# Hybrid attention and expert-retrieval step on one core: the planner that spreads the front's steps gives the choice of keys six row times instead of four

## The reference, cut to what matters

```python
h = rms(x)
cq, ckv, kpe, bq, bk, bv, iq, iw, ik, ga, gb = split(h @ w_in)
# mixer A: latent attention, 8 heads; mixer B: an indexer scores the keys, the best 128 of a prompt row are kept
score = einsum('bqh,bqhs->bqs', iw, relu(einsum('bqhd,bsd->bqhs', iq, ik)))
_, sel = top_k(where(mask, score, -inf), k_sel)
x = x + (sigmoid(ga) * (o_a @ w_o_a) + sigmoid(gb) * (o_b @ w_o_b)) @ w_out
# PEER: 8 heads, each takes 16 of 128*128 experts; u[e], v[e] are rows of 1024
a = gelu(einsum('td,thkd->thk', t, u[e]))
x = x + einsum('thk,thkd->td', g * a, v[e])
```

## Time and profile before

| | |
|---|---|
| time before, median of 3 runs | 1802.56 us (1797.75 to 1805.56) |
| the profiled execution's own time | 1796.99 us |
| its span | 1795.2 us |
| PE busy | 68% of the span |
| DVE busy | 73% |
| ACT busy | 32% |
| POOL busy | 29% |
| moved by DMA | 696.48 MB |

### The profile page before, as it was taken

How to read it: one execution, slowest core, us unless ns; L and a number is a source line. 1 busy time by engine, 2 the same in 40 slices (tenths; PEclk the granted TensorE clock), 3 DMA queues, 4 the chain that set the end, 5 groups by cost and what they waited for, 6 DMA issues and landing times.

```text
span 1795.2 us, 26399 instructions
## 1 busy us (share of the span) xinstructions
PE 1223.4 (68%) x9056; PEld 679.3 (38%) x9056; DVE 1310.8 (73%) x3857; ACT 579.7 (32%) x1995; POOL 526.2 (29%) x569
## 2 busy tenths in 40 slices
PE   8989976677867575878877666679867343434343
PEld 3668532344535232444535223356535111111111
DVE  5662696989666676989666768998766878686754
ACT  2331134333423333334323334344423222222222
POOL 0200232333322223332322223232323333333332
PEclk9989889787988696897998697887999555555555
DMA  6238699999999999999999999999999999999997
GB/s 267 74 100 294 250 422 421 422 425 425 424 424 423 417 401 383 420 425 424 425 423 422 423 407 390 426 400 398 422 424 423 427 426 426 425 427 423 427 421 294
DMA packets 119381, 696.48 MB, mean 388 GB/s; under 512 B 17983, under 2 KB 21118, under 8 KB 49102
## 3 DMA queue, kind: packets, MB, share of 16 engines
q0 software_dynamic: 78848, 570.53, 76.0%
q1 hardware_dynamic: 36686, 121.83, 17.5%
q10 hardware_dynamic: 3712, 2.43, 0.4%
HBM read 691.65 MB, written 3.02 MB: 387 GB/s over the span
## 4 chain that ended last, share of the span: by engine, by line
DMA 35%; DVE 25%; PE 25%; issue 6%; ACT 3%; POOL 1%; ACTq 0%; DVEq 0%; SPq 0%; POOLq 0%
DMA rows<-in_peer_uv,index 26%; DVE rows L2657 11%; PE ps_v L1820 5%; DMA wch<-in_w_row 4%; PE ps_f L1559 4%; PE ps_f L1353 2%; PE ps_f L1574 2%; PE ps_h L1800 2%; DMA wch<-in_peer_wq 2%; DVE score L2333 1%; PE ps_f L1477 1%; PE ps_f L1653 1%; DVE best L2332 1%; DMA wch<-in_w_ukv 1%; PE ps_f L1437 1%
## 5 line engine op out<-in xcount | busy, mean ns | idle before, releaser
L2657 DVE CUSTOM_DVE_ANT_0 rows<-rows,ps_h 128x1024 f32<-128x1024 f32 x544 | 658.0, 1220 | 289.1 <-DMA rows<-in_peer_uv,index 236.3
L1330 POOL DMA_INDIRECT rows<-in_peer_uv,index x544 | 516.4, 949 | 1169.4 <-PE ps_v L1820 988.8
L1820 PE MATMUL ps_v<-rows,diag 128*32 128x256 f32 x4352 | 419.1, 500 | 432.0 <-ACT diag L2164 424.8
L1820 PEld LDWEIGHTS ps_v<-rows,diag 128*32 128x32 f32 x4352 | 124.2, 130 | 677.5 <-ACT diag L2164 561.7
L2155 ACT ACTIVATE tan<-arg 128x2 f32<-128x2 f32 x272 | 55.3, 203 | 799.2 <-DVE arg L2667 756.4
L2158 ACT ACTIVATE weight<-tan,lead 128x1 f32<-128x1 f32 x544 | 180.8, 379 | 9.1
L2164 ACT ACTIVATE diag<-sel,weight 128x32 f32<-128x32 f32 x544 | 140.9, 306 | 0.6 <-PE ps_v L1820 0.6
L1559 PEld LDWEIGHTS ps_f<-bufh,wch 128*128 128x128 f32 x768 | 103.7, 214 | 19.9 <-issue 17.8
L1559 PE MATMUL ps_f<-bufh,wch 128*128 128x128 f32 x768 | 109.7, 302 | 0.0
L1353 PE MATMUL ps_f<-wch,bufh 128*128 128x512 f32 (+1 forms) x192 | 81.9, 565 | 27.7 <-DMA wch<-in_w_row 26.7
L1653 PE MATMUL ps_f<-bufh,wch 128*128 128x128 f32 x384 | 52.1, 293 | 12.5 <-DMA wch<-in_peer_wq 12.3
(11 more groups left out here) (398 smaller groups left out, 1682.4 us busy)
## 6 DMA issues: line engine op xcount, KB each, us to landing
wch<-in_w_gate SPq DMA_DIRECT2D x60, 512.0 KB
wch<-in_w_row SPq DMA_DIRECT2D x36, 512.0 KB
wch<-in_w_o SPq DMA_DIRECT2D x32, 512.0 KB
wch<-in_w_out SPq DMA_DIRECT2D x24, 512.0 KB
wch<-in_peer_wq SPq DMA_DIRECT2D x24, 512.0 KB
rows<-in_peer_uv,index POOLq DMA_INDIRECT x544
w_tok<-in_w_tok SPq DMA_DIRECT2D x4, 1640.0 KB, 12.9
wch<-in_w_uq SPq DMA_DIRECT2D x6, 384.0 KB
```

What stands on the lines that cost most here:

```text
L1330: pool.indirect_dma_start(rows[c % RING][:, :, :].rearrange("p a d -> p (a d)"), None, io.peer_uv[:, :], at).then_inc(s_uv[c % RING], 16)
L1820: ins = nc.tensor.matmul(ps_v[GROUP * a:GROUP * (a + 1), :], diag[:, c % DRING, :], rows[c % RING][:, 1, QD * a:QD * (a + 1)], start=False ...
L2657: v.tensor_tensor_reduce(out=u, in0=u, in1=ps_h[:, :], scale=1.0, scalar=0.0, op0=ALU.mult, op1=ALU.add, accum_out=dots[:, c % KEEP:c % KE ...
```

## The change

One factor in `step_work` goes from 4 to 6, so that a choice tick is costed at seven row times instead of five. No instruction is added or removed, and the same 117 ticks stand in the same order; only `spread_steps` gives other counts.

```diff
@@ -785,7 +785,7 @@
         if (u := unit_at(k, 2)) is not None and u < H:
             dve += row
         if (u := unit_at(k, 1)) is not None and u >= H:
-            dve += row + (4 * row if u < 2 * H else 0)
+            dve += row + (6 * row if u < 2 * H else 0)
         if unit_at(k, 7) in (2 * H - 1, UNITS - 1):
             dve += 0.9
         if k in (at.turn, at.rows, at.res) or at.mix <= k < at.mix + DC or at.ask <= k < at.ask + PH:
```

## The result

The changed kernel took 1805.61 us (median of 20 runs, 1800.87 to 1814.13) against 1798.69 us for the kernel before on the same chip (20 runs, 1794.54 to 1805.56). The ratio is 1.004, with a 95% interval of 1.003 to 1.0051. I had forecast 1798.1 us, 4.5 less than the median of before that I had; it came out 6.9 us more than the one beside it.

What follows compares the result with a forecast made beforehand. DMA's byte rate, about 425 GB/s, was taken to bound the kernel from 230 us on. Terms -2.8 - 1.9 - 0.8 - 0.7 + 1.7 = -4.5 us took the median 1802.56 to 1798.1 us; range 1788 to 1810.

Steps and rivals of the forecast that it cites:

- part 4: Behind the choice, window 1244 to 1260 us: ticks come a slot later, gaining 0.7 of 3.0 us lost.
- part 5: Ticks moved earlier crowd (pass 2's `up`, pass 3's slot 277): 1.7 us lost in one pass, bounds 0 and 7.4.
- Part 1: Pass 2's heads turn right behind their rotation, so spread and dot near 709 us come 2.8 us earlier.
- Part 2: Pass 3's heads turn earlier, during the wait for arguments ending at 1096.21 us: 1.9 us gained, low bound 0.
- Part 3: The choice gets more slots in each pass: 0.8 us gained of 2.4 lost at 1172 to 1200 us.
- C: Rival: `up` one dot sooner lets DMA run dry for one gather per pass, 7.4 us added, 1810.0 us; chance 0.14.
- A: Rival: lost time only moves, 1802.6 us; sign: both spread waits shorter, still 21 us or more lost; chance 0.24.
- B: Rival: the choice caused most loss; four of five windows close, all 14.8 us would give 1787.8; chance 0.10.

Runs made afterwards that it cites:

- pass 1 alone: Choice factor six in pass 1 only, four in passes 2 and 3, against the kernel before: ratio 0.9992 (0.9975 to 1.0008).
- the choice alone: Factor six only in the choice's slots (166 to 198 in pass 2, 290 to 326 in pass 3), against the kernel before: ratio 1.0006 (0.9992 to 1.002).
- the changed kernel again: The changed kernel, factor six in all passes, run and profiled a second time against the kernel before: 1803.8 us, ratio 1.0023 (1.0009 to 1.0037).

## Why the prediction was wrong, point by point

**The steps that failed** are part 4 and part 5. Part 4, "Behind the choice", says: "These ticks come a slot later, and one of its slots (339) is now empty. Of the 3.0 I take 0.7" as a gain. It looked only at the window that lost time before, took the steps' lateness there for a relief, and gave no price to pass 2, where slots 199 to 216 lost 0.1 us. It also read PE's "busy 16.00 of 16" without the clock, which was 0.50 for 4.4 of the 16 us. What it left out is a chain: DVE's division, PE's values and scores, DVE's logits. Moved two slots later alone, its first step brought DVE waits of 3.76 and 4.83 us and cost 1.0049. Before, in pass 2, DVE had three dots and a search beside the chain and didn't wait. Measured for the places: +4.3 and +3.1 us by the traces, 1.0022 and 1.0015 by the ratios (the second not told from 1), against my -0.7.

**Part 5, crowding, +1.7 for one pass, with a bound of 7.4:** right in sign, and as far off as part 4 by the traces: +3.0 in pass 1, +2.4 in pass 2 and +4.0 in pass 3, 9.4 us in all, over its bound. For pass 1 I had charged nothing as DMA was full there. The ratios don't show the size: pass 1 alone is 0.9992, and I have no reason for that.

**Part 1, pass 2's heads, -2.8:** right in mechanism. The wait for the spread fell from 5.62 to 2.93, and slots 158 to 166 lose 4.3 us less. The earlier `up` of the same pass, part 5, takes 2.4 of it back. The ratio of the two together, 1.001, shows no gain; with an interval from 0.9995 it rules out more than 0.9 us.

**Part 2, pass 3's heads, -1.9:** right at its place too, -2.0 us in slots 284 to 290; the wait for the spread fell by 1.3 us. But 4.0 us more are lost ahead of it, where the crowded slots 277 and 282 lie, and 1.8 behind it. The slower spread, 3.78 us, costs no DMA time that the traces show. The heads' ratio is 1.0013, not told from 1.

**Part 3, the choice, -0.8:** nothing of it shows. Pass 2's choice loses no time in either kernel, pass 3's changes by +0.2; the ratio is 1.0006.

**The rivals.** C had 0.14 and was right on most of what part 5 missed. It said that `up` one dot earlier lets DMA run dry for one gather, 2.47 us, in each pass, with a dip below 400 GB/s in pass 1 or 2 as its sign. The dips are there (394 and 324 GB/s), and the traces lose 3.0 and 2.4 us more. The wait for `up` itself hardly grew (7.08 to 7.31 us in pass 2); by C's argument it counts that it comes a dot sooner. In pass 3 `up` did not move, and the crowding of slot 277 did the like. C was wrong in that the gains of the turns would not show, and it had nothing behind the choice. A described where pass 2's head ends well: the dot behind it is where it was, counted from the first dot (499.8 us before, 499.7 after), since pass 1 had lost what the heads won; and its sign, both waits shorter but 21 us or more lost from 230 us on, holds with 36.7. But the time did not stay. B, the choice, was not there at all.

**The base.** I set the forecast against a median of three runs, 1802.56; the runs beside the changed kernel had 1798.69. This is 3.9 us of the 7.5 between forecast and result that have nothing to do with the change.

**What stays open.** The parts nearly add, pass by pass (0.9992, 1.0018, 1.0033), but not at two points: one moved step costs as much as the whole change, and the changed kernel with the old places behind the choice is not faster (1.0046). So the new places behind the choice are enough to cost time, but they are not shown to be what makes the changed kernel slower. The traces of the kernel with the old places there and of that with the choice alone show the wait in another slot of pass 3, so it seems that the place of a chain is good or bad only together with the slots ahead of it. Which one is good I can't work out from the steps alone. No kernel has `up` in its old slot and the turns in their new ones, so C's term is told by the traces alone, and its price in the time isn't known. The clock's share isn't separated either: my added matmuls did not hold it high where it counted. No version beat the kernel before by more than its interval.

## What to carry to other kernels

A planner's cost is a price and also moves everything behind it: look for the chains that go from one engine to another and back, see what covers each now, and ask whether the new slot has that cover too, above all where no time is lost today. A window in which an engine is busy all the time says nothing before its clock and its counts of instructions are read beside it. And where the steps lie in a pattern (here a part of `choose` in every second slot), one step two slots later can cost more (7.6 us here) than the gain that a whole redistribution was forecast to bring (4.5).

## What the runs showed of the hardware

Between 230 and 1400 us PE's clock stood at its lower level, 0.50, in 33 stretches of the profiled execution of before and in 43 of the changed kernel's, and the same matmuls then took about twice as long: the sixteen of L1559 2.05 and 3.78 us, the scores of L1437 0.94 and 1.70, the spread 1.98 and 3.78. Stretches lie at places at which PE waited (3.15 us ahead of 845.93 in the changed kernel, with the clock low from 845.5 us), but 1.93 us of added small matmuls in such a wait, which left 1.29 us of it, did not keep it up in pass 2. The Trainium skill (TensorE: Matmul & The Clock Gate, HAM oscillation) describes this: a wait for data lets the clock fall, and the next burst of work starts slow. The traces agree in that; that the filled gap didn't help isn't covered by it.

Not all low stretches recur: of the two profiles of the changed kernel, one has two between 700 and 730 us and the other none, while both have one from 845.5 to 855.9. Runs with a lower mean clock tend to be longer: in the kernel with the one step moved later, from 1800.62 us at 0.784 to 1811.21 at 0.771. But at the same clock of about 0.78 the medians of the kernels still differ as their ratios do (1803.8 for the changed kernel again, 1797.58 for the kernel before with added matmuls), so the mean clock doesn't account for the difference between kernels. Whether it spreads the runs of one kernel, or is lower because PE waited more in them, isn't shown.
